# Spreading 28 groups of background slabs over eight loop iterations instead of seven, in a one-layer RWKV and block-attention step

## The chip, the core and the metric

The kernel runs on one core of a Trainium2 chip. The metric is the device time of one execution in microseconds (us). TensorE (PE) does the matmuls, with its weight loads (PEld) beside them; VectorE (DVE) and ScalarE (ACT) do the elementwise work and move results out of PSUM; GpSimd (POOL) does a little; SyncE (SP) issues nearly all DMAs, in program order.

## The reference, cut to what matters

One decoder layer is computed for 288 tokens (256 of a prompt, 8 sequences of 4). The normalised input `h` (288 x 2048) goes through one projection whose columns are split:

```
h = _rmsnorm(x, norm1_g) * (1 + scale1) + shift1       # scale, shift, gate: silu(c) @ w_ada
z = h @ w_in                                           # columns: z_a | q_b k_b v_b | gate_a gate_b
o_a = rwkv7(z_a) @ w_proj_a                            # 16 heads of 64, state recurrence
o_b = moba(rope(q_b), rope(k_b), v_b, cache) @ w_proj_b   # 8 heads of 128, paged keys and values
mix = sigmoid(gate_a) * o_a + sigmoid(gate_b) * o_b
x = x + gate1 * (mix @ w_out)                          # then a ConvFFN and a last norm
```

## The kernel before, in words

The stages run one after the other: adaLN and norm; `za` (the columns `z_a`); then eight iterations j = 0 to 7 of `rwkv(j)`, each for one pair of RWKV heads; then rotary and attention over the paged cache; then merge, out, up and down.

An RWKV iteration is a long chain of small steps that PE, ACT, DVE and POOL hand to each other (log decays, pair products, seven levels of a triangular inverse, two chunks of state, group norm). Two kinds of background work are threaded through it by hand, as every engine's order is the program's:

- **ada slabs.** `ada(j, p)`, p = 0 to 7, uses two 512 KB slabs of `w_ada` each, 16 per iteration, straight from the ring `raw`.
- **fill slabs.** The remaining 56 tiles of 128 columns of `w_in` (q_b, k_b, v_b, gates) are computed in 28 groups of two tiles. A group has four slabs of 512 KB. For each slab ACT makes `whi` (`rest_hi`), DVE makes `wlo` (`rest_lo`), and PE does 24 matmuls in two halves (`rest(j, i, 0)` and `rest(j, i, 1)`). After four slabs ACT copies two PSUM banks to `restev` (`rest_evac`) and stores them to `spill` in DRAM (`rest_spill`). `fill(i)` places slab i at its point of an iteration. Slabs 0 to 11 lie ahead of `ada(j, 6)`; slab 12 lies on both sides of the samples' state update, slab 13 around the turning of the final states, slab 14 around the two sums of the group norm, slab 15 at the very end.

Iterations 0 to 6 are `dense`: 4 groups, 16 fill slabs. Iteration 7 has none. Fill and ada slabs share the four places of the ring (fill in 1 and 3, ada in 0 and 2) in iterations 0 to 6; iteration 7 uses all four for ada. `rest_hi(j, RS)` and `rest_lo(j, RS)` prepare the next iteration's slab 0 near the end of an iteration, for j < 6.

An ada slab's load waits until the slab two before it is used. At an iteration's end the DVE does, in order: group norm's centring and squares (L1712, L1713), `fill(15)`, the next pair's `mix_pair`, then a reciprocal and four products, `yalo` (`ya_lo`), a small add to `mod`, the next slab's `rest_lo`, and then the next iteration's `v_kk` and `v_sq` (L1601, L1602). The next iteration on PE begins with four matmuls on `lora` and one pair on `v_sq`, ahead of its fill slab 0.

In iteration 7 SP also loads what attention needs first. The gates (32 of the spilled tiles, 4 DMAs, L740) are put where `hhi` and `hlo` lay, so they wait for the last fill slab; key pages 4 to 7 (L722) are put where `whi` and `wlo` lie, behind the last ada slab; `pair_stores` stores the pair's states (L694, L697). After the loop SP waits for `ya_lo`, for all the state stores and for the gates, and loads the heads' q, k and v from `spill` (`heads_load`, L747 and L748); `rotate(0)` on PE waits for the first head.

Of the kernel before, what the change touches and what calls it, by code (L numbers as in the profile page):

```python
# [31 lines left out]
P = 128  # L32
# [6 lines left out]
DB, HB, HEAD_B = 1024, 8, 128  # L39
KA = DA // P  # L40
# [14 lines left out]
CH = 512  # L55
# [77 lines left out]
def build(nc, d):  # L133
    ctx = ExitStack()
    with ctx:  # L135
# [397 lines left out]
        ADA_J = (ADA_G - ADA_1) // KA * ADA_K  # L533
        assert ADA_J == 16
        N_XT, N_T = 2 * LEVELS - 3, 2 * LEVELS - 2
        ADA_ROWS1 = 1
# [50 lines left out]
        def _(sp):  # L587
# [86 lines left out]
            def rest_slab(j, i):  # L674
                r, n = 1 + 2 * (i % 2), stages["rest"][0] + i
                src = d["w_in"][i % 4 * CH:i % 4 * CH + CH, bass.ds(j * (RG * RW) + (ZA + i // 4 * RW), RW)].rearrange("(t p) n -> p t n", p=P)
                sp.wait_ge(slab_lo, j * RS + (n - 1))
                sp.dma_start(quads(raw[:, r, :, :]), src).then_inc(slab_in[r], 16)

            def both_slabs(j, s0, s1):  # L680
                for s in range(s0, s1):
                    rest_slab(j, s)
                    ada_slab(j, s)
# [14 lines left out]

            with sp.Fori(0, 1) as j:
                both_slabs(j, 0, 3)  # L700
                lora_loads(j)
                both_slabs(j, 3, 13)
                state_loads(j)
                both_slabs(j, 13, RS)
            with sp.Fori(1, KA - 1) as j:
                both_slabs(j, 0, 3)
                lora_loads(j)
                both_slabs(j, 3, 6)
                pair_stores(j - 1)
                both_slabs(j, 6, 13)  # L710
                state_loads(j)
                both_slabs(j, 13, RS)

# [9 lines left out]

            j = KA - 1
            n1 = stages["merge"][0]
            for s in range(ADA_J):
                idx = ADA_1 * ADA_K + j * ADA_J + s
                src = wsrc(d["w_ada"], s % ADA_K * 2 * P, j * (2 * CH) + (ADA_1 + s // ADA_K) * CH, CH)
                if s < 4:
                    wait = ((ada_used, idx - 1), (slab_lo, n1 - 1), (ada_used, idx - 2), (slab_lo, n1))[s]  # L730
                else:
                    wait = (ada_used, idx - 3)
                slab(s, 0, 0, src, wait)
                if s == 5:
                    pair_stores(j - 1)
                if s == 9:
                    sp.wait_ge(spilled, 16 * RG * (KA - 1))
                    sp.wait_ge(slab_used, n1)
                    for q in range(4):
                        sp.dma_start(gt[:, 8 * q:8 * q + 8, :], spill[3 * HB + 8 * q:3 * HB + 8 * q + 8, :, :].rearrange("t p f -> p t f")).then_inc(reloaded, 16)  # L740
            sp.wait_ge(states_in, 48)
            pages("cache_k", 0, None, None, range(4, NPG))
            pair_stores(KA - 1)

# [68 lines left out]
        def landed(name, g, s):  # L813

            n0, ks, _ = stages[name]
            up0 = stages["up"][0]
            n = n0 + ks * g.c + s
            before = (ADA_1 if name == "za" else ADA_G) * ADA_K - ADA_RAW
            v, per = 16 * (before // 4 + n // 4 + 1), 4
            if name == "up":  # L820
                v, per = v + 16 * ((n - up0) // 4 + 1), 8
            if name == "down":
                v += 16 * (stages["down"][0] - up0) // 4
            return v if g.i is None else g.i * (g.a * ks * per) + v
# [114 lines left out]
        def _(act):  # L939
# [110 lines left out]
            def rest_hi(j, i):  # L1050
                r, n = 1 + 2 * (i % 2), stages["rest"][0] + i
                act.wait_ge(slab_in[r], j * (RS * 8) + 16 * (REST_IN + i // 2 + 1))
                act.wait_ge(slab_used, j * RS + (n - 1))
                copy(whi[:, n % 2, :, :], raw[:, r, :, :]).then_inc(slab_hi, 1)

            def rest_evac(j, q):
                act.wait_ge(slab_used, j * RS + (stages["rest"][0] + 4 * q + 4))
                act.wait_ge(spilled, j * (16 * RG) + 16 * q)
                copy(restev[:, :, :], ps[:, 5:7, 0:T]).then_inc(rest_out, 1)

            def rest_spill(j, q):
                act.wait_ge(rest_out, j * RG + (q + 1))
                act.dma_start(spill[one(j, 2, 2 * RG, 2 * q), :, :].rearrange("t p f -> p t f"), restev[:, :, :]).then_inc(spilled, 16)

# [4 lines left out]

            def rwkv(j, dense, more):  # L1070
                jc = one(j)
                w0h, a0h = smallc[:, one(j)], smallc[:, one(j, off=8)]

                def fill(i):
                    if dense:
                        rest_hi(j, i)
# [29 lines left out]
                copy(BN[0:m, 2, :], pbank(4)[0:m, 2 * P:3 * P], scale=-1.0).then_inc(rows_done, 1)  # L1106
                if dense:
                    rest_evac(j, 0)
                fill(5)

                for lev in range(1, LEVELS):
# [9 lines left out]
                    if lev == LEVELS - 1:  # L1121
                        act.wait_ge(t_done, j * N_T + N_T - 1)
                        for h in (slice(0, 64), slice(64, P)):
                            copy(Tf[h, :, :, h].rearrange("p e c t -> p (e c) t"), TT[h, :, :, :].rearrange("p e c t -> p (e c) t"))
                    if lev == 1 and dense:
                        rest_spill(j, 0)
                    if lev == 4 and dense:
                        rest_evac(j, 1)
                    if lev == 5 and dense:
                        rest_spill(j, 1)  # L1130
# [29 lines left out]
                right_sides(1)  # L1160
                if dense:
                    rest_evac(j, 2)
                fill(13)
                solved(1)
                if dense:
                    rest_spill(j, 2)
                fill(14)
# [13 lines left out]
                act.activation(v_px[:, :], pbank(0)[:, 0:T], ACT.Sqrt, bias=c("eps_lnx"), scale=1.0 / HEAD_A).then_inc(gn_roots, 1)  # L1181
                if more:
                    rest_hi(j, RS)
                act.wait_ge(ya_done, j + 1)
                act.activation(yahi[:, jc, :].rearrange("p o t -> p (o t)"), v_thw[:, :], ACT.Copy).then_inc(branch_hi, 1)
                if dense:
                    rest_evac(j, 3)
                    rest_spill(j, 3)
# [5 lines left out]
            for j in range(KA):  # L1194
                rwkv(j, j < KA - 1, j < KA - 2)

# [162 lines left out]
        def _(dve):  # L1359
# [227 lines left out]
            def rest_lo(j, i):  # L1587
                r, n = 1 + 2 * (i % 2), stages["rest"][0] + i
                dve.wait_ge(slab_hi, j * RS + (n + 1))
                TTn(wlo[:, n % 2, :, :], raw[:, r, :, :], whi[:, n % 2, :, :].bitcast(F32), ALU.subtract).then_inc(slab_lo, 1)  # L1590

            def rwkv(j, dense, more):

                def fill(i):
                    if dense:
                        rest_lo(j, i)
# [130 lines left out]
                ada_cols(2 * j + (ADA_1 + 1), 2 * j + (ADA_1 + 2), 7)  # L1727
                if more:
                    rest_lo(j, RS)

# [3 lines left out]
            for j in range(KA):  # L1734
                rwkv(j, j < KA - 1, j < KA - 2)

# [232 lines left out]
        def _(pe):  # L1969
# [178 lines left out]
            def ada(j, p):  # L2148

                for s in (2 * p, 2 * p + 1):  # L2150
                    if s % ADA_K == 0:
                        pe.wait_ge(ada_in_mod, 2 * j + (ADA_1 + s // ADA_K))
                    if isinstance(j, int) and j == KA - 1:
                        r = s % 4
                        pe.wait_ge(slab_in[r], 16 * (REST_IN + 8 * j + s // 4 + 1))
                    else:
                        r = 2 * (s % 2)
                        pe.wait_ge(slab_in[r], j * (RS * 8) + 16 * (REST_IN + s // 2 + 1))
                    for kt in range(2):
                        t = 2 * (s % ADA_K) + kt  # L2160
                        strip = slice(ADA_W * (t % 4), ADA_W * (t % 4) + ADA_W)
                        i = mm(pbank(7)[strip, :], scT[:, t, :], raw[:, r, kt, :], t < 4, t >= KD - 4)
                    i.then_inc(ada_used, 1)

            def rest(j, i, half):

                n = stages["rest"][0] + i
                if half == 0:
                    pe.wait_ge(slab_lo, j * RS + (n + 1))
                    if i % 4 == 0:  # L2170
                        pe.wait_ge(rest_out, j * RG + i // 4)
                wh, wl = quads(whi[:, n % 2, :, :]), quads(wlo[:, n % 2, :, :])
# [10 lines left out]

            def rwkv(j, dense):

                def fill(i, half):
                    if dense:
                        rest(j, i, half)
# [258 lines left out]
            for j in range(KA):  # L2447
                rwkv(j, j < KA - 1)

# [227 lines left out]
```

## Time and profile before

| | us |
|---|---|
| median of 3 runs (2392.01 to 2397.01) | 2396.04 |
| the profiled execution | 2395.43 |
| its span | 2393.6 |
| RWKV iterations 0 to 6, mean | 101.8 |
| iteration 7 (from 984.50) to `rotate(0)` at 1060.99 | 76.5 |

Times in a view are counted from the span's start. An iteration is named by its j, 0 to 7. In a timeline a row is one group of like instructions: start, length, engine, line, operation, output and inputs; in square brackets how long the engine sat idle before it and what it waited for. A matmul's length contains the time for its result to drain, so the distance of two starts tells more.

### The profile page before, as it was taken

The page shows a single profiled execution, that of the slowest core. Times are in us where ns is not written, and L with a number is a line of the kernel's source. Part 1 is how long each engine was busy: PE and PEld are TensorE (multiplying, and loading weights), DVE is VectorE, ACT ScalarE, POOL GpSimd, SP SyncE. Part 2 cuts the span into 40 slices and gives each one's busy share as a digit, 9 for nine tenths or more (in the row PEclk, how much of TensorE's full clock was granted, in tenths as well). Part 3 has the DMA queues.
Part 4 walks back from the last instruction along what each step waited for, and adds up shares of the span by engine and source line. Part 5 has one row for each costly group of instructions (what it writes and reads, how often), then busy time and mean ns, then how long its engine had stood idle before and what let it go on. Part 6 is the DMA issues. An engine that isn't in the chain of part 4 may idle for free. (4 is left out here: it accounts for less than half of the span.)

```text
span 2393.6 us, 49529 instructions
## 1 busy us (share of the span) xinstructions
PE 2282.3 (95%) x19772; PEld 2018.1 (84%) x19772; DVE 1150.5 (48%) x1904; ACT 959.4 (40%) x1413; POOL 105.5 (4%) x224
## 2 busy tenths in 40 slices
PE   6999899999999999878998999799999999999998
PEld 3889787887878788646666999799999999999998
DVE  4456635445353543434444555655544554544443
ACT  2433424334333343326452333354545545433333
POOL 0000011000000000100000000000100100000000
PEclk8999999999999999969998999999999999999999
DMA  9885556565665656667995455355555555555543
GB/s 332 307 290 147 159 182 184 177 196 179 187 189 177 183 177 190 216 207 252 390 384 185 150 161 166 98 167 167 165 163 163 165 167 166 163 166 164 160 149 117
DMA packets 326691, 461.20 MB, mean 193 GB/s; under 512 B 37337, under 2 KB 220395, under 8 KB 326075
## 3 DMA queue, kind: packets, MB, share of 16 engines
q1 hardware_dynamic: 318312, 450.22, 58.5%
q10 hardware_dynamic: 8215, 8.59, 1.1%
q8 instruction: 128, 2.10, 0.4%
q14 instruction: 36, 0.29, 0.0%
HBM read 442.86 MB, written 15.86 MB: 192 GB/s over the span
## 5 line engine op out<-in xcount | busy, mean ns | idle before, releaser
L942 ACT ACTIVATE whi<-raw 128x1024 fp32r<-128x1024 f32 (+1 forms) x512 | 526.3, 1028 | 910.8 <-PE ps L1973 880.9
L1973 PE MATMUL ps<-hhi,whi 128*128 128x288 f32 x2736 | 832.2, 304 | 10.0 <-DVE hlo L1456 6.4
L1973 PE MATMUL ps<-hhi,wlo 128*128 128x288 f32 x2736 | 807.9, 295 | 0.0
L1973 PE MATMUL ps<-hlo,whi 128*128 128x288 f32 x2736 | 807.2, 295 | 0.0
L1405 DVE TENSOR_TENSOR wlo<-raw,whi 128x1024 fp32r<-128x1024 f32 (+1 forms) x400 | 470.2, 1177 | 639.2 <-ACT whi L942 639.1
L1973 PEld LDWEIGHTS ps<-hhi,whi 128*128 128x128 f32 x2736 | 514.8, 188 | 72.5 <-issue 52.0
L1973 PEld LDWEIGHTS ps<-hlo,whi 128*128 128x128 f32 x2736 | 515.3, 188 | 1.2
L1973 PEld LDWEIGHTS ps<-hhi,wlo 128*128 128x128 f32 x2736 | 514.8, 188 | 0.0
L1973 PE MATMUL ps<-fhi,whi 128*128 128x288 f32 x704 | 208.0, 295 | 2.8 <-DVE wlo L1405 2.8
L1973 PE MATMUL ps<-fhi,wlo 128*128 128x288 f32 x704 | 207.7, 295 | 0.0
L1973 PE MATMUL ps<-flo,whi 128*128 128x288 f32 x704 | 207.3, 294 | 0.0
L1590 DVE TENSOR_TENSOR wlo<-raw,whi 128x1024 fp32r<-128x1024 f32 x112 | 136.7, 1220 | 101.8 <-ACT whi L942 101.6
L1973 PEld LDWEIGHTS ps<-fhi,whi 128*128 128x128 f32 x704 | 132.1, 188 | 3.6 <-DVE wlo L1405 3.5
L1973 PEld LDWEIGHTS ps<-flo,whi 128*128 128x128 f32 x704 | 132.1, 188 | 0.2
L1973 PEld LDWEIGHTS ps<-fhi,wlo 128*128 128x128 f32 x704 | 132.1, 188 | 0.0
L1973 PE MATMUL ps<-raw,scT 128*32 128x512 f32 x512 | 79.5, 626 | 5.6 <-DMA raw<-in_w_ada 5.6
L1973 PE MATMUL ps<-mhi,whi 128*128 128x288 f32 x256 | 76.4, 298 | 1.6 <-DVE wlo L1405 1.6
L942 ACT ACTIVATE Xs<-ps 128x256 f32<-128x256 f32 (+1 forms) x48 | 18.4, 383 | 143.3 <-PE ps L1973 143.1
L1973 PE MATMUL ps<-mlo,whi 128*128 128x288 f32 x256 | 75.7, 296 | 0.0
L1973 PE MATMUL ps<-mhi,wlo 128*128 128x288 f32 x256 | 75.2, 294 | 0.0
L942 ACT ACTIVATE kT<-ps 128x1024 f32<-128x1024 f32 x64 | 64.6, 1021 | 25.9 <-PE ps L2516 25.7
L1674 DVE TENSOR_TENSOR Tn<-Tn,ps 128x128 f32<-128x128 f32 x40 | 11.5, 288 | 122.2 <-PE ps L1973 122.2
(393 smaller groups left out, 2758.1 us busy)
## 6 DMA issues: line engine op xcount, KB each, us to landing
raw<-in_w_up SPq DMA_DIRECT2D x352, 256.0 KB, 2.9
raw<-in_w_ada SPq DMA_DIRECT2D x128, 512.0 KB, 4.8
raw<-in_w_in SPq DMA_DIRECT2D x112, 512.0 KB, 4.5
raw<-in_w_down SPq DMA_DIRECT2D x88, 512.0 KB, 3.8
kpage<-in_cache_v SPq DMA_DIRECT2D x64, 512.0 KB, 5.8
raw<-in_w_in SPq DMA_DIRECT2D x72, 384.0 KB, 5.6
kpage<-in_cache_k SPq DMA_DIRECT2D x40, 512.0 KB, 5.3
ada_d<-in_w_ada SPq DMA_DIRECT2D x32, 512.0 KB, 5.8
```

What stands on the lines that cost most here:

```text
L942: return act.activation(o, i, ACT.Copy, **k)
L1405: TTn(wlo[:, n % 2, :, 0:width], raw[:, n % 4, :, 0:width], whi[:, n % 2, :, 0:width].bitcast(F32), ALU.subtract).then_inc(slab_lo, 1)
L1590: TTn(wlo[:, n % 2, :, :], raw[:, r, :, :], whi[:, n % 2, :, :].bitcast(F32), ALU.subtract).then_inc(slab_lo, 1)
L1674: TTn(even, even, pbank(1)[:, 0:2 * H].rearrange("p (n t) -> p n t", t=1 << lev), ALU.subtract).then_inc(t_done, 1)
L1973: return pe.matmul(out, lhsT, rhs, start=start, stop=stop, **k)
```

## The change

`GROUPS = [4, 3, 4, 3, 4, 3, 4, 3]` gives the groups of each iteration. Odd iterations, the last among them, have fill slabs 0 to 11 only; the total stays 28. The counts of all semaphores follow. SP's two loops become one unrolled loop over all eight iterations; iteration 7 has the same ring places as the others. Gates and key pages 4 to 7 are issued after iteration 7's last ada slab, the pages first, once the last fill slab is used and spilled. The next iteration's slab 0 is prepared for all j < 7.

```diff
+        GROUPS = [4, 3, 4, 3, 4, 3, 4, 3]
+        G_0 = [sum(GROUPS[:j]) for j in range(KA + 1)]
...
             def both_slabs(j, s0, s1):
                 for s in range(s0, s1):
-                    rest_slab(j, s)
+                    if s < 4 * GROUPS[j]:
+                        rest_slab(j, s)
                     ada_slab(j, s)
...
-            with sp.Fori(0, 1) as j:
...
-            with sp.Fori(1, KA - 1) as j:
+            for j in range(KA):
                 both_slabs(j, 0, 3)
-                lora_loads(j)
+                if j < KA - 1:
+                    lora_loads(j)
                 both_slabs(j, 3, 6)
-                pair_stores(j - 1)
+                if j:
+                    pair_stores(j - 1)
                 both_slabs(j, 6, 13)
-                state_loads(j)
-                both_slabs(j, 13, RS)
+                if j < KA - 1:
+                    state_loads(j)
+                both_slabs(j, 13, ADA_J)
...
-            for s in range(ADA_J):
...
-                if s == 9:
-                    sp.wait_ge(spilled, 16 * RG * (KA - 1))
-                    sp.wait_ge(slab_used, n1)
-                    for q in range(4):
-                        sp.dma_start(gt[:, 8 * q:8 * q + 8, :], spill[3 * HB + 8 * q:3 * HB + 8 * q + 8, :, :].rearrange("t p f -> p t f")).then_inc(reloaded, 16)
             sp.wait_ge(states_in, 48)
+            sp.wait_ge(slab_used, stages["merge"][0])
             pages("cache_k", 0, None, None, range(4, NPG))
+            sp.wait_ge(spilled, 16 * G_0[KA])
+            for q in range(4):
+                sp.dma_start(gt[:, 8 * q:8 * q + 8, :], spill[3 * HB + 8 * q:3 * HB + 8 * q + 8, :, :].rearrange("t p f -> p t f")).then_inc(reloaded, 16)
             pair_stores(KA - 1)
...
                 def fill(i):
-                    if dense:
+                    if i < 4 * GROUPS[j]:
                         rest_hi(j, i)
...
-                if more:
-                    rest_hi(j, RS)
+                if j < KA - 1:
+                    rest_hi(j + 1, 0)
...
-                if dense:
+                if GROUPS[j] > 3:
                     rest_evac(j, 3)
                     rest_spill(j, 3)
```

DVE and PE get the same `if i < 4 * GROUPS[j]` for `fill`.

## Rows read from the trace of the kernel before

**Rows 1.** The page: TensorE's granted clock in 40 slices of the span.

```profile
PEclk8999999999999999969998999999999999999999
```

**Rows 2.** Windows: length, busy time by engine, then granted clock, DMA share, GB/s.

```profile
883.18:984.50 101.32, 99.92 (x1016) 82.07 (x1015) 46.38 (x85) 36.38 (x66) 6.94 (x11) 1.00 0.61 186
886.14:963.33 77.19, 76.64 (x853) 63.68 (x854) 33.09 (x60) 28.15 (x54) 5.27 (x10) 1.00 0.63 188
...
986.54:1038.42 51.88, 43.41 (x567) 28.76 (x566) 17.87 (x47) 14.14 (x39) 5.46 (x12) 0.83 0.80 264
1038.42:1061.00 22.58, 12.78 (x62) 6.51 (x58) 7.86 (x16) 4.28 (x7) 0.00 (x0) 0.65 0.20 50
1004.00:1024.00 20.00, 16.19 (x282) 12.33 (x284) 4.80 (x15) 4.69 (x12) 2.45 (x5) 0.83 1.06 357
```

**Rows 3.** Timeline of PE: marks of iterations 6 and 7 and the attention's start.

```profile
886.14 0.75 PE L1973 MATMUL ps<-v_sq,cst 128*128 128x288 f32 x2 [0.85 <-DVE v_sq L1602]
...
986.54 0.75 PE L1973 MATMUL ps<-v_sq,cst 128*128 128x288 f32 x2
...
1038.42 1.98 PE L1973 MATMUL ps<-Vblk,KN 32*64 32x512 f32 x4
...
1060.99 2.26 PE L1973 MATMUL ps<-qk,cst 128*128 128x288 f32 x4 [8.76 <-DMA vq<-spill]
```

**Rows 4.** Timeline of PE: iteration 6 behind `ada(6, 6)`.

```profile
965.12 1.08 PE L1973 MATMUL ps<-Vblk,KN 32*64 32x512 f32 x4
...
966.99 0.34 PE L1973 MATMUL ps<-VN,KN 128*64 128x64 f32 x4
...
969.10 0.40 PE L1973 MATMUL ps<-hhi,whi 128*128 128x288 f32 x1
...
972.40 0.27 PE L2428 MATMUL ps<-cst,SE 128*64 128x128 f32 x1
...
973.47 1.07 PE L1973 MATMUL ps<-raw,scT 128*32 128x512 f32 x8
...
976.17 0.65 PE L1973 MATMUL ps<-v_thw,cst 128*128 128x288 f32 x2
```

**Rows 5.** Timeline of DVE: ends of iterations 5 and 6.

```profile
884.10 1.22 DVE L1590 TENSOR_TENSOR wlo<-raw,whi 128x1024 fp32r<-128x1024 f32 x1
...
885.63 0.46 DVE L1602 TENSOR_TENSOR v_sq<-v_kk 128x288 f32<-128x288 f32 x1
...
977.35 0.46 DVE L1713 TENSOR_TENSOR v_sq<-v_ld 128x288 f32<-128x288 f32 x1
...
978.86 0.48 DVE L1561 SCALAR_TENSOR_TENSOR rkv<-dif,par,za 128x256 f32<-128x256 f32 x1
...
980.53 1.95 DVE L1718 RECIPROCAL v_px<-v_px 128x288 f32<-128x288 f32 x1
...
985.31 0.19 DVE L1397 TENSOR_TENSOR mod<-ps,par 128x36 f32<-128x36 f32 x1
```

**Rows 6.** Timeline of PE: iteration 0 starts after an idle stretch.

```profile
271.90 1.33 PE L1973 MATMUL ps<-lw,lora 64*128 64x288 f32 x4 [4.64 <-ACT nshn L942]
...
281.42 0.27 PE L2204 MATMUL ps<-cst,v_ld 128*128 128x128 f32 x1
```

**Rows 7.** Timeline of SP: its DMA issues.

```profile
963.56 0.37 SPq L672 DMA_DIRECT2D raw<-in_w_ada  x1
...
1003.88 8.52 SPq L740 DMA_DIRECT2D gt<-spill  x4
...
1048.56 5.16 SPq L697 DMA_DIRECT2D out_wkv_sample<-stout  x8
...
1056.90 0.83 SPq L747 DMA_DIRECT2D qk<-spill  x2
```

**Rows 8.** DMA issues from 984 to 1062: KB each, median us to landing.

```profile
raw<-in_w_ada SPq DMA_DIRECT2D x12, 512.0 KB, 4.7
gt<-spill SPq DMA_DIRECT2D x4, 1152.0 KB, 12.9
```

More of the change, by code:

```diff
@@ L534, in build @@
         assert ADA_J == 16
+        GROUPS = [4, 3, 4, 3, 4, 3, 4, 3]
+        G_0 = [sum(GROUPS[:j]) for j in range(KA + 1)]
+        assert G_0[KA] == RG * (KA - 1)
         N_XT, N_T = 2 * LEVELS - 3, 2 * LEVELS - 2
@@ L675, in rest_slab @@
                 r, n = 1 + 2 * (i % 2), stages["rest"][0] + i
-                src = d["w_in"][i % 4 * CH:i % 4 * CH + CH, bass.ds(j * (RG * RW) + (ZA + i // 4 * RW), RW)].rearrange("(t p) n -> p t n", p=P)
-                sp.wait_ge(slab_lo, j * RS + (n - 1))
+                src = d["w_in"][i % 4 * CH:i % 4 * CH + CH, bass.ds(ZA + (G_0[j] + i // 4) * RW, RW)].rearrange("(t p) n -> p t n", p=P)
+                sp.wait_ge(slab_lo, 4 * G_0[j] + (n - 1))
                 sp.dma_start(quads(raw[:, r, :, :]), src).then_inc(slab_in[r], 16)
@@ L697, in pair_stores @@
                     sp.dma_start(d["wkv_sample"][b, one(j, 2, 2), :, :].rearrange("h v k -> v h k"), stout[:, b, :, :]).then_inc(sstate_out, 16)
-            with sp.Fori(0, 1) as j:
+            for j in range(KA):
                 both_slabs(j, 0, 3)
-                lora_loads(j)
-                both_slabs(j, 3, 13)
-                state_loads(j)
-                both_slabs(j, 13, RS)
-            with sp.Fori(1, KA - 1) as j:
-                both_slabs(j, 0, 3)
-                lora_loads(j)
+                if j < KA - 1:
+                    lora_loads(j)
                 both_slabs(j, 3, 6)
-                pair_stores(j - 1)
+                if j:
+                    pair_stores(j - 1)
                 both_slabs(j, 6, 13)
-                state_loads(j)
-                both_slabs(j, 13, RS)
+                if j < KA - 1:
+                    state_loads(j)
+                both_slabs(j, 13, ADA_J)
             def pages(cache, R, used, value, which=range(NPG), apart=False):
@@ L722, in pages @@
                     sp.dma_start(place, d[cache][bass.ds(page, 1), :, :, :].rearrange("o p h f -> p (o h f)")).then_inc(landed_, 16)
-            j = KA - 1
-            n1 = stages["merge"][0]
-            for s in range(ADA_J):
[L727 to L735, printed above, removed]
-                if s == 9:
-                    sp.wait_ge(spilled, 16 * RG * (KA - 1))
-                    sp.wait_ge(slab_used, n1)
-                    for q in range(4):
-                        sp.dma_start(gt[:, 8 * q:8 * q + 8, :], spill[3 * HB + 8 * q:3 * HB + 8 * q + 8, :, :].rearrange("t p f -> p t f")).then_inc(reloaded, 16)
             sp.wait_ge(states_in, 48)
+            sp.wait_ge(slab_used, stages["merge"][0])
             pages("cache_k", 0, None, None, range(4, NPG))
+            sp.wait_ge(spilled, 16 * G_0[KA])
+            for q in range(4):
+                sp.dma_start(gt[:, 8 * q:8 * q + 8, :], spill[3 * HB + 8 * q:3 * HB + 8 * q + 8, :, :].rearrange("t p f -> p t f")).then_inc(reloaded, 16)
             pair_stores(KA - 1)
@@ L819, in landed @@
             v, per = 16 * (before // 4 + n // 4 + 1), 4
+            if name != "za":
+                v += 16 * (KA * ADA_J // 2 - 2 * G_0[KA]) // 2 * (1 if n % 2 == 0 else -1)
             if name == "up":
@@ L1051, in rest_hi @@
                 r, n = 1 + 2 * (i % 2), stages["rest"][0] + i
-                act.wait_ge(slab_in[r], j * (RS * 8) + 16 * (REST_IN + i // 2 + 1))
-                act.wait_ge(slab_used, j * RS + (n - 1))
+                act.wait_ge(slab_in[r], 16 * (REST_IN + 2 * G_0[j] + i // 2 + 1))
+                act.wait_ge(slab_used, 4 * G_0[j] + (n - 1))
                 copy(whi[:, n % 2, :, :], raw[:, r, :, :]).then_inc(slab_hi, 1)
             def rest_evac(j, q):
-                act.wait_ge(slab_used, j * RS + (stages["rest"][0] + 4 * q + 4))
-                act.wait_ge(spilled, j * (16 * RG) + 16 * q)
+                act.wait_ge(slab_used, stages["rest"][0] + 4 * (G_0[j] + q) + 4)
+                act.wait_ge(spilled, 16 * (G_0[j] + q))
                 copy(restev[:, :, :], ps[:, 5:7, 0:T]).then_inc(rest_out, 1)
             def rest_spill(j, q):
-                act.wait_ge(rest_out, j * RG + (q + 1))
-                act.dma_start(spill[one(j, 2, 2 * RG, 2 * q), :, :].rearrange("t p f -> p t f"), restev[:, :, :]).then_inc(spilled, 16)
+                act.wait_ge(rest_out, G_0[j] + q + 1)
+                act.dma_start(spill[one(G_0[j] + q, 2, 2), :, :].rearrange("t p f -> p t f"), restev[:, :, :]).then_inc(spilled, 16)
             def ada_rows2(j, half):
@@ L1068, in ada_rows2, with rwkv @@
                 copy(adr[:, :], pbank(7)).then_inc(ada_copied, 1)
-            def rwkv(j, dense, more):
+            def rwkv(j):
                 jc = one(j)
@@ L1106, in rwkv @@
                 copy(BN[0:m, 2, :], pbank(4)[0:m, 2 * P:3 * P], scale=-1.0).then_inc(rows_done, 1)
-                if dense:
-                    rest_evac(j, 0)
+                rest_evac(j, 0)
                 fill(5)
@@ L1124, in rwkv @@
                             copy(Tf[h, :, :, h].rearrange("p e c t -> p (e c) t"), TT[h, :, :, :].rearrange("p e c t -> p (e c) t"))
-                    if lev == 1 and dense:
+                    if lev == 1:
                         rest_spill(j, 0)
-                    if lev == 4 and dense:
+                    if lev == 4:
                         rest_evac(j, 1)
-                    if lev == 5 and dense:
+                    if lev == 5:
                         rest_spill(j, 1)
@@ L1160, in rwkv @@
                 right_sides(1)
-                if dense:
-                    rest_evac(j, 2)
+                rest_evac(j, 2)
                 fill(13)
                 solved(1)
-                if dense:
-                    rest_spill(j, 2)
+                rest_spill(j, 2)
                 fill(14)
@@ L1181, in rwkv @@
                 act.activation(v_px[:, :], pbank(0)[:, 0:T], ACT.Sqrt, bias=c("eps_lnx"), scale=1.0 / HEAD_A).then_inc(gn_roots, 1)
-                if more:
-                    rest_hi(j, RS)
+                if j < KA - 1:
+                    rest_hi(j + 1, 0)
                 act.wait_ge(ya_done, j + 1)
                 act.activation(yahi[:, jc, :].rearrange("p o t -> p (o t)"), v_thw[:, :], ACT.Copy).then_inc(branch_hi, 1)
-                if dense:
+                if GROUPS[j] > 3:
                     rest_evac(j, 3)
@@ L1194, in _ @@
             for j in range(KA):
-                rwkv(j, j < KA - 1, j < KA - 2)
+                rwkv(j)
             def plain(name, u=None, added=None, ends={}):
@@ L1588, in rest_lo, with rwkv @@
                 r, n = 1 + 2 * (i % 2), stages["rest"][0] + i
-                dve.wait_ge(slab_hi, j * RS + (n + 1))
+                dve.wait_ge(slab_hi, 4 * G_0[j] + (n + 1))
                 TTn(wlo[:, n % 2, :, :], raw[:, r, :, :], whi[:, n % 2, :, :].bitcast(F32), ALU.subtract).then_inc(slab_lo, 1)
-            def rwkv(j, dense, more):
+            def rwkv(j):
                 def fill(i):
-                    if dense:
+                    if i < 4 * GROUPS[j]:
                         rest_lo(j, i)
@@ L1727, in rwkv @@
                 ada_cols(2 * j + (ADA_1 + 1), 2 * j + (ADA_1 + 2), 7)
-                if more:
-                    rest_lo(j, RS)
+                if j < KA - 1:
+                    rest_lo(j + 1, 0)
             own(dve.memset(Tf[64:P, :, :, 0:64], 0.0))
@@ L1734, in _ @@
             for j in range(KA):
-                rwkv(j, j < KA - 1, j < KA - 2)
+                rwkv(j)
             def fl(ap):
@@ L2152, in ada @@
                         pe.wait_ge(ada_in_mod, 2 * j + (ADA_1 + s // ADA_K))
[L2153 to L2158, printed above, removed]
+                    r = 2 * (s % 2)
+                    pe.wait_ge(slab_in[r], 16 * (REST_IN + j * (ADA_J // 2) + s // 2 + 1))
                     for kt in range(2):
@@ L2168, in rest @@
                 if half == 0:
-                    pe.wait_ge(slab_lo, j * RS + (n + 1))
+                    pe.wait_ge(slab_lo, 4 * G_0[j] + (n + 1))
                     if i % 4 == 0:
-                        pe.wait_ge(rest_out, j * RG + i // 4)
+                        pe.wait_ge(rest_out, G_0[j] + i // 4)
                 wh, wl = quads(whi[:, n % 2, :, :]), quads(wlo[:, n % 2, :, :])
@@ L2182, in rest, with rwkv @@
                     ins.then_inc(slab_used, 1)
-            def rwkv(j, dense):
+            def rwkv(j):
                 def fill(i, half):
-                    if dense:
+                    if i < 4 * GROUPS[j]:
                         rest(j, i, half)
@@ L2447, in _ @@
             for j in range(KA):
-                rwkv(j, j < KA - 1)
+                rwkv(j)
+            pe.wait_ge(rest_out, G_0[KA])
             pe.wait_ge(ya_lo, KA)
```

## The prediction, made before the changed kernel ran

> **What bounds the kernel now.** I read the page's slices first, then windows over single iterations, then the timelines of PE, DVE and SP around the places that the change touches. The slices [rows 1] show TensorE at its full clock nearly everywhere, with one dip in the middle. The windows place it: iteration 6 runs at clock 1.00 with PE busy for 99.9 of 101.3 us, while in iteration 7 the clock is 0.83 and PE is busy for 43.4 of 51.9 us up to the mark of 1038.42, and then 0.65 and 12.8 of 22.6 us up to the start of attention [rows 2]. So the dense iterations are bound by PE's queue of work, and the one without fill slabs by its own chain of small steps, partly at half clock. Moving PE work into iteration 7 fills that hole. The question is what the iterations that give it up lose, and what the later loads cost.
>
> Three marks divide the time. V(j) is the start of the `v_sq` matmuls at an iteration's beginning, at 886.14 for j = 6 and 986.54 for j = 7 [rows 3]. A(j) is the end of `ada(j, 6)`: behind it the fill slabs 12 to 15 are placed; it is 963.33 for j = 6 [rows 2] and 1038.42 for j = 7 [rows 3]. R is the distance from A(7) to `rotate(0)`, 1060.99 - 1038.42 = 22.6 us now [rows 3].
>
> **Step 1, iteration 7 gets twelve fill slabs.** V to A becomes as long as in iteration 6, whose first twelve slabs are the same: 77.2 us in place of 51.9 [rows 2], so +25.3 us. Twelve slabs at 3.3 us (two halves from 969.10 to 972.40 [rows 4]) are 39.6 us of PE work, so about 14 us of it go into idle time and slow clock. This is the whole gain of the change.
>
> **Step 2, slab 0 of iteration 7.** The end of iteration 6 now prepares it as the ones before did. In iteration 6 PE waited 0.85 us for DVE's `v_sq` [rows 3], 2.96 us after the iteration's start at 883.18 [rows 2]; iteration 7 reached the mark 2.04 us after 984.50. That is +0.9 us.
>
> **Step 3, the three tails without slabs 12 to 15 (j = 1, 3, 5).** Now A(6) to the next V takes 984.50 - 963.33 + 2.96 = 24.1 us. What it takes without fill is a chain through three engines, which I lay out from A. The samples' update on PE takes 966.99 - 965.12 = 1.9 us, chunk results 969.10 - 966.99 = 2.1, turning the states 973.47 - 972.40 = 1.1, `ada(j, 7)` another 1.1 [rows 4]: 6.2 us. The load of the last ada slab goes out about 0.9 us after A (the one before it leaves 0.23 after A, at 963.56 [rows 7]) and lands 4.7 us later [rows 8], at 5.6 us; PE wants it at about 5.7, so it may be just late, by a few tenths. Group norm: from the first sum's matmul at 976.17 [rows 4] to the end of DVE's squares at 977.81 [rows 5] are 1.6 us: 7.8. `mix_pair` takes 980.53 - 978.86 = 1.7 (PE's second sum and ACT's root lie beside it): 9.5. Reciprocal to `mod`, 985.31 - 980.53 = 4.8: 14.3. Then 0.1 for `mod`, and from the start of the next `rest_lo` to the end of `v_sq` 886.09 - 884.10 = 2.0 [rows 5]: 16.4 us, and with a tenth for the ada slab 16.5. PE's own work ends earlier: the next V is set by DVE, and PE stands some 4 us idle ahead of it, having only the `lora` matmuls to do. So a tail saves 24.1 - 16.5 = 7.6 us, though it gives up 12.9 us of PE work (21.2 us of the tail less its own 8.3 of small steps). I take 7.5, three times: -22.5 us. The bounds are 6.5 (the ada slab a full microsecond late) and 12.9 (no new stall). The evacuation and spill that fall away lie beside PE and cost nothing either way; SP's unrolling changes no order.
>
> **Step 4, from A(7) to attention.** Before, gates and key pages were loaded beside iteration 7. Now SP can send them only after the last ada slab's load, 0.9 us after A. Behind A stand two ada slabs (1.05 MB), four pages of 512 KB (2.1 MB) and the gates, 4 x 1152 KB = 4.72 MB [rows 8]: 7.9 MB. While the gates were loaded before, all DMA engines were busy and moved 357 GB/s [rows 2], so this takes 22.0 us and ends at about A + 23 to 24, with the time in which the first bytes come into motion. The last state stores are issued behind the gates; SP needs 5.2 us for them [rows 7] and they are done at about A + 24.3. The heads' loads wait for both, and `rotate(0)` came 1060.99 - 1056.90 = 4.1 us after the first of them was issued [rows 3, 7]. So R becomes 28.4 us, +5.8. Compute alone would be ready earlier: `ya_lo` comes at about A + 13.8 (7.8, then 1.2 for sum and root, 4.8 for the DVE's products), so R is at least 17.9. The upper bound is 32, if SP cannot issue its stores before the queue has drained (its four gate issues took 8.5 us before [rows 7]) and stores and landing follow the gates in series.
>
> The pattern speaks against spreading as such: an iteration of 4 groups hides its chain fully; one of 3 loses 5.3 us (12.9 - 7.6), and four such lose 21 us, whereas the empty iteration lost about 17 (the 76.5 us to `rotate(0)` less the 8.8 us of idle time before it [rows 3] are 67.7; an iteration's own steps without fill and waits are about 101.3 - 4 x 12.9 = 50).
>
> **Rivals.**
>
> *The clock falls in the short tails.* Each has an idle stretch of some 4 us behind light work. Iteration 0 shows what that costs: after 4.64 us idle, 9.5 us pass from its first matmul to the transposes of `v_ld` [rows 6], where 2.0 + 0.8 + 3.3 = 6.1 are needed at full clock. That is 3.4 us, three times: +10.3, 2415 us. For it: that one gap is of the size expected here. Against it: the stretch V to A of iteration 7, light work all through, still had a mean clock of 0.83 [rows 2], and a short tail is much shorter. I give it 0.2. The Trainium skill ("TensorE: Matmul & The Clock Gate", Why this matters for your kernels) warns of idle gaps between bursts of matmuls, behind which the clock is low again; by that rule this is the likely case and the sum would be 2415. The trace agrees in the one place that has such a gap.
>
> *The later loads are hidden.* If the transfers end before `ya_lo`, R is 17.9 in place of 28.4. The total is 9.5 - 10.5 = -1.0: 2394 us, no difference. It needs 7.9 MB in 13 us, about 600 GB/s, against 357 seen; or that the heads don't wait for the gates, which the code excludes. Chance 0.12.
>
> *The tails cost nothing.* If DVE's chain overlapped with the next iteration's first slab and PE never waited, each tail would save all 12.9 us: 25.3 + 0.9 - 38.7 + 5.8 = -6.7, 2389 us, faster. It decides from 10.7 us saved per tail on, that is a new stall below 2.2 us. Against it stands the order of PE's queue, where fill slab 0 lies behind the matmuls on `v_sq`, and that even the dense tail is 0.85 us short [rows 3]. Chance 0.09.
>
> That the change does nothing is no case: it moves 12 slabs.
>
> **How the numbers follow.** The case above has a chance of 0.55, with its own range from 2400 (tails save 8.5, R 26.5) to 2411 (6.5 and 31). The clock has 0.2, the hidden loads 0.12, the free tails 0.09, and 0.04 is left for what I don't see, more of it slow. The range 2395 to 2416 leaves out the free tails, part of the hidden loads, and the worst of the clock case. A measurement of this kernel tells about 0.2% (4.8 us) from no change. Within it fall the hidden loads and the lower edge of the main case, 0.15; faster 0.1; slower 0.75.
>
> **What would show it.** Right: distance V to V of 101 us for even j and 94 for j = 1, 3, 5; PE idle for 4 us or more ahead of the `v_sq` matmuls in iterations 2, 4 and 6, put down to DVE's L1602; A(7) at about 986.5 + 0.9 - 22.5 + 77.2 = 1042, 4 us later than before; DMA engines full for 20 us behind it; `rotate(0)` at about 1070 after an idle stretch of more than 15 us, put down to the heads' DMA. Wrong: short tails of 89 to 91 us (free), or of 97 and more with a clock below 1.00 (throttled); `rotate(0)` less than 20 us behind A(7); or a change of length behind `rotate(0)`, on which I set nothing.

## The result, and the profile after

The changed kernel takes 2407.98 us (median of 4 runs, 2402.84 to 2413.03) against 2394.3 us of the kernel before, run beside it. The ratio is 1.0055, with a 95% interval of 1.0040 to 1.0071: slower by 0.55%, where 0.4% had been forecast (2405 us). The profiled execution is the fastest of the four, 2402.84 us with a span of 2401.0 us, 7.4 us above the profiled one of before. Its V(0) also lies 3.5 us earlier than in the trace shown before (272.15 against 275.68), ahead of everything that the change touches, so the distances between marks tell more than the totals.

Windows of the changed kernel: iterations 1 and 2 from V to V, V to A of iteration 7, A(7) to `rotate(0)`, and 20 us inside that. They answer to [rows 2].

```profile
375.28:468.78 93.50, 87.31 (x918) 69.33 (x918) 41.53 (x82) 33.31 (x63) 8.04 (x11) 0.98 0.58 175
468.78:571.28 102.50, 101.24 (x1015) 83.21 (x1015) 46.20 (x85) 36.96 (x66) 8.04 (x11) 0.99 0.60 184
965.05:1040.65 75.60, 75.60 (x854) 63.55 (x854) 30.54 (x58) 26.23 (x52) 6.56 (x12) 1.00 0.53 166
1040.65:1071.66 31.01, 8.49 (x61) 4.77 (x58) 7.87 (x16) 4.17 (x7) 0.00 (x0) 0.68 0.92 297
1044.00:1064.00 20.00, 5.14 (x35) 3.11 (x32) 6.54 (x15) 4.17 (x7) 0.00 (x0) 0.70 1.06 360
```

Iteration 7 is now filled: 75.6 us at full clock with PE never idle. Iteration 1, with three groups, lasts 93.5 us and PE is busy for 87.3 of them. Behind A(7) PE has 8.5 us of work in 31.0 us, while the DMA engines are full.

Timeline of PE from A(1), at 452.21, over the bare end of iteration 1, and around A(7) and `rotate(0)`; the latter two answer to [rows 3].

```profile
452.21 1.08 PE L1960 MATMUL ps<-Vblk,KN 32*64 32x512 f32 x4
...
460.32 0.75 PE L1960 MATMUL ps<-v_sq,cst 128*128 128x288 f32 x2 [1.04 <-DVE v_sq L1700]
460.91 0.95 PE L1960 MATMUL ps<-cst,adr 128*128 128x9 f32 x8
461.80 0.76 PE L1960 MATMUL ps<-lw,lora 64*128 64x288 f32 x4
...
468.78 1.33 PE L1960 MATMUL ps<-v_sq,cst 128*128 128x288 f32 x2 [4.87 <-DVE v_sq L1589]
...
1040.65 1.08 PE L1960 MATMUL ps<-Vblk,KN 32*64 32x512 f32 x4
...
1071.66 2.26 PE L1960 MATMUL ps<-qk,cst 128*128 128x288 f32 x4 [21.48 <-DMA vq<-spill]
```

From A(1) to V(2) pass 16.6 us. PE waits 4.87 us of them for DVE's `v_sq`, and the pair on it then takes 1.33 us in place of the 0.75 in [rows 3]: TensorE is at its lower clock (1.2 GHz). Windows of 1 us place the fall, first in the tail of iteration 1, then in that of iteration 3:

```profile
463.00:464.00 1.00, 0.91 (x3) 0.29 (x2) 0.96 (x2) 0.00 (x0) 0.00 (x0) 1.00 1.04 379
464.00:465.00 1.00, 0.00 (x0) 0.00 (x0) 0.93 (x3) 0.00 (x0) 0.00 (x0) 0.90 0.23 80
465.00:466.00 1.00, 0.00 (x0) 0.00 (x0) 0.71 (x2) 0.22 (x1) 0.00 (x0) 0.50 0.00 0
659.00:660.00 1.00, 1.00 (x6) 0.35 (x5) 1.00 (x3) 0.84 (x1) 0.00 (x0) 0.68 1.13 387
```

PE's wait begins at 463.9, and the clock falls about 1 us into it. In iteration 3 it falls between 659 and 660 with PE at work, some 3 us ahead of that tail's wait, which is then 3.37 us long. Timeline of DVE in the same stretch, which answers to [rows 5]:

```profile
459.81 0.46 DVE L1700 TENSOR_TENSOR v_sq<-v_ld 128x288 f32<-128x288 f32 x1
...
461.86 1.95 DVE L1705 RECIPROCAL v_px<-v_px 128x288 f32<-128x288 f32 x1
...
466.63 0.19 DVE L1384 TENSOR_TENSOR mod<-ps,par 128x36 f32<-128x36 f32 x1
466.74 1.22 DVE L1577 TENSOR_TENSOR wlo<-raw,whi 128x1024 fp32r<-128x1024 f32 x1
467.87 0.36 DVE L1588 TENSOR_SCALAR v_kk<-rkv,par 128x288 f32<-128x288 f32 x1
468.27 0.46 DVE L1589 TENSOR_TENSOR v_sq<-v_kk 128x288 f32<-128x288 f32 x1
```

From the start of the group norm's squares to the end of the next `v_sq`, 468.73, DVE has one gap, 0.51 us ahead of `yalo` for ACT's `yahi`, and otherwise none above a few hundredths: the wait is that chain. Timeline of SP behind A(7), which answers to [rows 7]:

```profile
1042.73 3.72 SPq L723 DMA_DIRECT2D kpage<-in_cache_k  x4
1046.49 9.98 SPq L730 DMA_DIRECT2D gt<-spill  x4
1056.52 3.23 SPq L698 DMA_DIRECT2D out_wkv_prompt<-stp  x1
1059.80 5.16 SPq L701 DMA_DIRECT2D out_wkv_sample<-stout  x8
1067.78 0.81 SPq L735 DMA_DIRECT2D qk<-spill  x2
```

The prompt state's store, which took 0.63 us to issue in the kernel before, takes 3.23 here, and the eight stores of the sample states go out at 1059.8, 19 us behind A. The heads' loads begin 27.1 us behind A.

| distance | before | after | forecast |
|---|---|---|---|
| V to V, j = 1, 3, 5 | 101.3, 101.3, 101.9 | 93.5, 94.8, 93.5 | 94 |
| V to V, j = 2, 4, 6 | 101.1, 101.6, 100.4 | 102.5, 102.4, 103.1 | 101 (j = 6: 101.3) |
| V(7) to A(7) | 51.9 | 75.6 | 77.2 |
| A(7) to `rotate(0)` | 22.6 | 31.0 | 28.4 |
| `rotate(0)` to the span's end | 1332.6 | 1329.4 | the same |

### The profile page after: what moved, and what is told of

It reads as the page before. It is cut to its first block and busy times, and to the rows that moved or that the text cites. A ratio compares the mean times of both kernels' runs of the same rounds, so it can differ in the third digit from the quotient of the medians.

```text
span 2401.0 us, 48785 instructions
## 1 busy us (share of the span) xinstructions
PE 2275.6 (95%) x19772; PEld 2015.8 (84%) x19772; DVE 1149.8 (48%) x1904; ACT 959.3 (40%) x1413; POOL 113.2 (5%) x224
## 5 line engine op out<-in xcount | busy, mean ns | idle before, releaser
L932 ACT ACTIVATE Xs<-ps 128x256 f32<-128x256 f32 (+1 forms) x48 | 18.4, 383 | 144.1 <-PE ps L1960 143.9
```

Of the source, the lines that this page charges most:

```text
L932: return act.activation(o, i, ACT.Copy, **k)
```

## The experiments

`all_in_seven`, `no_gates`, `warm` and `squares_early` ran beside 21 runs of the kernel before (median 2393.82 us), the other four beside 24 (2394.99 us).

**The groups of before with the loads of after.** `all_in_seven`:

```diff
-        GROUPS = [4, 3, 4, 3, 4, 3, 4, 3]
+        GROUPS = [4, 4, 4, 4, 4, 4, 4, 0]
...
```

The rest of the diff takes away the copies, the spills and the prepared slab 0 of a group that isn't there.

> The changed kernel with the groups of before (4 in seven iterations, none in the last): no short tail and no fill in iteration 7, but gates and first key pages still behind the last ada slab. Theory (the tails cost about 6 us each with the clock, the late loads about 8 us): iterations 0 to 6 last 101.3 us again, the A mark of iteration 7 is 52 to 58 us behind V, because its ada slabs now have two places in the ring, R is about 30 us in place of 22.6, and the kernel needs 2402 to 2409 us, slower than before by 8 us or more. Rival (the late loads are harmless, the short tails are the whole loss): 2393 to 2397 us, as before.

Measured: 2407.58 us, ratio 1.0051 (1.0034 to 1.0068). Windows from V(7) to A(7) and on to `rotate(0)`:

```profile
981.67:1044.51 62.84, 52.81 (x566) 37.06 (x565) 17.89 (x47) 14.16 (x39) 5.46 (x12) 0.65 0.35 110
1044.51:1075.84 31.33, 13.15 (x61) 6.49 (x58) 7.87 (x16) 4.28 (x7) 0.00 (x0) 0.61 0.88 287
```

R is 31.3 us without any fill in iteration 7 and without a short tail: the late loads cost 8.7 us by themselves. V to A is longer than expected, 62.8 us: against [rows 2] PE is busy 9.4 us more with the same 566 matmuls, at a mean clock of 0.65 in place of 0.83. Iterations 1 to 5 last 100.6 to 101.4 us. So the loss of the late loads is real and separate, and an empty last iteration is worse beside them than it was. The trace shows where that begins. The same stretch in three windows, and the instruction that holds up DVE, and PE behind it, in the second:

```profile
981.67:997.00 15.33, 12.03 (x129) 7.10 (x128) 9.18 (x21) 7.72 (x19) 2.07 (x6) 1.00 0.57 166
997.00:1001.00 4.00, 1.07 (x11) 0.16 (x8) 1.44 (x5) 0.00 (x0) 0.21 (x1) 0.91 0.51 114
1001.00:1044.51 43.51, 39.71 (x429) 29.80 (x429) 7.27 (x22) 6.44 (x20) 3.18 (x6) 0.50 0.27 89
```

```profile
999.56 1.42 DVE L1644 TENSOR_TENSOR Rm<-ps,cst 128x256 f32<-128x256 f32 x4 [3.99 <-DMA out_wkv_sample<-stout]
```

DVE waits 3.99 us for the stores of the pair before, which SP issues behind the iteration's first six ada slabs; PE then stands idle for 3.97 us, and the clock is at 0.50 from there to A(7). In the trace of before DVE doesn't wait at that place. The sample states' stores go out 10.4 us behind V(7) here, against 4.8 before, when the ada slabs had four places in the ring and not two. So the ring places have a part in it; no run takes them back alone.

**One short tail.** `one_short`:

```diff
-        GROUPS = [4, 3, 4, 3, 4, 3, 4, 3]
+        GROUPS = [4, 4, 4, 4, 4, 4, 3, 1]
...
```

> The changed kernel with groups 4, 4, 4, 4, 4, 4, 3, 1: one short tail, and one group in the last iteration. Theory: iterations 1 to 5 last 101.3 us, iteration 6 about 93.7, iteration 7 loses 0.5 to 1.5 us at half clock at its start, its V to A lasts 66 to 70 us (its first four slabs, then the small steps with the ada slabs in two places), R is 31 as in the changed kernel. The total is that of the groups-as-before kernel less 13 us for the group moved out of iteration 6, plus 5 to 6 for the tail, plus 4 to 8 in iteration 7: 2403 to 2410. Rival (the loss is that of the late loads alone and short tails are free): below 2400.

Measured: 2405.2 us, ratio 1.0046 (1.0031 to 1.0060).

```profile
879.57:972.64 93.07, 87.16 (x918) 69.32 (x919) 41.57 (x82) 33.31 (x63) 6.90 (x11) 0.99 0.58 176
972.64:1039.85 67.21, 62.93 (x662) 46.98 (x662) 21.14 (x50) 16.50 (x41) 5.46 (x12) 0.75 0.38 119
```

Iterations 1 to 5 are back at 100.8 to 101.3 us and the one short iteration lasts 93.1: the loss belongs to each short tail and not to the change as a whole. R is 30.2 us.

**Without the gates' loads.** `no_gates` leaves them out, with the waits on them lowered to match. The sigmoids read the layer's input in their place, so the outputs are not the layer's:

```diff
-            for q in range(4):
-                sp.dma_start(gt[:, 8 * q:8 * q + 8, :], spill[3 * HB + 8 * q:3 * HB + 8 * q + 8, :, :].rearrange("t p f -> p t f")).then_inc(reloaded, 16)
...
```

> The changed kernel without the four loads of the gates; the sigmoids read the layer's input in their place, so the merge gets other factors. Theory (the heads wait behind 4.7 MB of gates): R falls from 31 to 18 to 22 us, and the kernel gains 9 to 13 us, to about 2396. Rival (R is set by the state stores' own wait and by SP's issuing of pages and stores): R stays above 26, and the gain is below 5 us.

Measured: 2394.14 us, ratio 1.0011 (0.9997 to 1.0025). R is 18.4 us:

```profile
1041.41:1059.85 18.44, 8.55 (x62) 4.79 (x58) 7.86 (x16) 4.17 (x7) 0.00 (x0) 0.77 0.77 244
```

SP issues the sample states' stores at 1048.0, 6.6 us behind A in place of 19.2, and the heads at 1055.9. So the gates' 4.7 MB are the whole of the loss behind A: R is 12.6 us shorter than in the changed kernel, and near the 17.9 that the prediction gave as the least.

**Idle matmuls in the wait.** `warm` puts 32 matmuls whose result is overwritten ahead of the `v_sq` pair behind each short tail:

```diff
+                if j and GROUPS[j - 1] < 4:
+                    pe.wait_ge(rest_out, G_0[j])
+                    for _ in range(32):
+                        mm(pbank(5)[:, 0:T], hhi[:, 0, 0:P], hhi[:, 1, :])
                 pe.wait_ge(kk_squares, j + 1)
```

> The changed kernel with 32 idle matmuls on PE (into the bank of the next fill group, overwritten later) in the wait ahead of v_sq behind each short tail: some 4.3 us of work in a 4.9 us wait. Theory (the idle stretch brings the clock to half for a few us, which costs 1.3 us in each following iteration): the clock stays at 1.00 there, iterations 2, 4 and 6 last 101.3 in place of 102.6 us, and the kernel gains 3 to 4 us, about 2403 to 2405. Rival (the longer even iterations have another cause, such as a later slab): their length stays at 102.6 with the clock at 1.00.

Measured: 2399.52 us, ratio 1.0023 (1.0013 to 1.0032). Timeline of PE, and the two iterations' windows:

```profile
463.58 4.52 PE L1960 MATMUL ps<-hhi 128*128 128x288 f32 x32
468.52 0.75 PE L1960 MATMUL ps<-v_sq,cst 128*128 128x288 f32 x2 [0.42 <-DVE v_sq L1589]
```

```profile
375.07:468.52 93.45, 91.99 (x950) 73.61 (x950) 41.53 (x82) 33.35 (x63) 8.07 (x11) 1.00 0.57 175
468.52:569.78 101.26, 99.93 (x1014) 82.08 (x1014) 46.23 (x85) 36.97 (x66) 6.94 (x11) 1.00 0.61 186
```

The short iteration keeps its length, since DVE sets it; the clock stays at 1.00 up to A(7), the pair takes 0.75 us again, and the even iterations last 101.3, 101.0 and 101.1 us in place of 102.5, 102.4 and 103.1. That is 1.2, 1.4 and 2.1 us, 1.6 on average and 4.7 in all. The whole gained 7.7 us by the ratios (0.32%), more than the 3 to 4 expected, and the two intervals leave 2 to 14 us. From V(0) to V(7) the two traces differ by 5.8 us, so a further 1.1 lies in the other iterations, most of it in iteration 3; the rest I can't place, and the changed kernel's runs lie 10 us apart.

**DVE's order.** `squares_early`:

```diff
                 if j < KA - 1:
                     mix_pair(j, 1)
+                    dve.wait_ge(gn_vars, j + 1)
+                    kk_start(j + 1)          # v_kk and v_sq of the next pair
+                    rest_lo(j + 1, 0)
                 dve.wait_ge(gn_roots, j + 1)
...
-                if j < KA - 1:
-                    rest_lo(j + 1, 0)
```

> The changed kernel with one order changed on DVE: the next pair's v_kk and v_sq and the next fill slab 0's low part come right behind mix_pair, ahead of the reciprocal and the four products. Theory (the short tail is set by DVE's chain ahead of v_sq): the 4.9 us wait of PE ahead of the v_sq matmuls goes, about 1 us of it comes back at v_ld, a short iteration lasts 89 to 91 us in place of 93.9, the clock no longer falls behind it, the dense boundaries lose their 0.85 us; all in all 13 to 18 us less, about 2391. Rival (the tail is set by the ada slabs' loads or by the sum of many small waits): short iterations stay within 1 us of 93.9 and the gain is 0.85 us per boundary at most, 5 us in all.

Measured: 2415.07 us, ratio 1.0089 (1.0072 to 1.0106): slower, against both expectations. The longest waits of PE over the RWKV stage and into attention, in us: total, number, longest one.

```profile
PE ps L1964 <- DMA vq<-spill: 23.5, 3, 21.5
PE ps L1964 <- DVE wlo L1577: 15.1, 7, 2.7
...
PE ps L2191 <- DVE v_ld L1594: 3.7, 3, 3.3
```

The wait ahead of `v_sq` is gone at all seven boundaries, and a wait for slab 1's low part has taken its place at all seven. Timelines of DVE, ACT and PE at the start of iteration 2 show why:

```profile
470.33 0.46 DVE L1718 TENSOR_TENSOR yalo<-v_thw,yahi 128x288 fp32r<-128x288 f32 x1 [0.51 <-ACT yahi L1172]
...
476.04 1.23 DVE L1577 TENSOR_TENSOR wlo<-raw,whi 128x1024 fp32r<-128x1024 f32 x1 [1.14 <-ACT whi L932]
```

```profile
470.87 1.28 ACT L1070 ACT_TABLE_LOAD   x1 [0.57 <-DVE yalo L1718]
472.16 0.50 ACT L1070 ACTIVATE v_thw<-ps,smallc 128x288 f32<-128x288 f32 x1
...
474.96 1.05 ACT L932 ACTIVATE whi<-raw 128x1024 fp32r<-128x1024 f32 x1
```

```profile
473.06 0.33 PE L2191 MATMUL ps<-cst,v_ld 128*128 128x128 f32 x1 [0.20 <-DVE v_ld L1594]
477.32 0.40 PE L1964 MATMUL ps<-hhi,whi 128*128 128x288 f32 x1 [2.72 <-DVE wlo L1577]
```

ACT's tanh must wait for `yalo`, because both use `v_thw`; slab 1's `whi` is queued behind tanh and root on ACT. Moving two products and a slab ahead of `yalo` made that path 2 us later: `yalo` begins 8.6 us behind the group norm's squares in place of 6.5. Every boundary has the wait, 2.0 us behind a dense iteration and 1.5 to 2.7 behind a short one. The short iteration did shrink, 93.5 to 92.85 us, and the next one grew from 102.5 to 105.5; the mark between them moved, so their sum tells more, 198.3 us in place of 196.0. V(7) to A(7) grew too, from 75.6 to 80.1. The wait had two loops through DVE behind it, and the edit relieved one at the cost of the other.

The clock fell here as well, and not behind a long wait. At the end of iteration 1 PE has stood idle for 1.04 us only, up to 462.29:

```profile
464.00:465.00 1.00, 1.00 (x5) 0.56 (x4) 0.95 (x3) 0.52 (x1) 0.00 (x0) 0.73 1.10 392
465.00:466.00 1.00, 1.00 (x3) 0.29 (x2) 1.00 (x2) 0.00 (x0) 0.00 (x0) 0.50 1.04 376
```

It also fell behind five of the seven waits for slab 1, three of them 2.0 us long at the start of iterations 1, 3 and 7.

**Other slabs left out.** `spread` keeps the last slabs in iterations 1, 3 and 5 and leaves out positions 6, 8, 10 and 12; the evacuation of the second group moves to where slab 12 was on ACT, and that of the third to the iteration's end:

```diff
+        KEEP = [list(range(16)) if g == 4 else [0, 1, 2, 3, 4, 5, 7, 9, 11, 13, 14, 15] for g in GROUPS]
+        KEEP[KA - 1] = list(range(12))
...
-                    if i < 4 * GROUPS[j]:
-                        rest(j, i, half)
+                    if i in KEEP[j]:
+                        rest(j, KEEP[j].index(i), half)
...
```

> The changed kernel, but iterations 1, 3 and 5 leave out fill positions 6, 8, 10 and 12 in place of 12 to 15: the same twelve slabs, with three of them at the end over DVE's chain. Theory (a short iteration loses 5 to 7 us only because its end is bare): a short iteration lasts 89 to 91 us in place of 93.9, PE waits 0.85 us ahead of v_sq as behind a dense one, the clock stays at 1.00 and the even iterations are back at 101.3; 12 to 18 us less than the changed kernel, 2390 to 2395. Rival (any four slabs left out expose as much, since the engines' small steps bind everywhere once PE has less to do): short iterations stay at 93 us or more, with waits at the places left out, and the time stays above 2402.

Measured: 2392.01 us, ratio 0.9996 (0.9978 to 1.0014), the time of the kernel before. The two windows of iterations 1 and 2, and PE's waits over the RWKV stage and into attention:

```profile
375.12:464.67 89.55, 87.23 (x919) 69.48 (x919) 41.45 (x81) 32.54 (x62) 8.59 (x11) 1.00 0.60 183
464.67:566.69 102.02, 99.92 (x1015) 82.08 (x1015) 46.28 (x85) 37.43 (x67) 8.06 (x11) 1.00 0.60 184
```

```profile
PE ps L1968 <- DMA vq<-spill: 22.5, 3, 21.1
PE ps L1968 <- DVE v_sq L1597: 5.9, 7, 0.8
PE ps L1968 <- DMA raw<-in_w_ada: 4.7, 8, 1.3
...
PE ps L1968 <- ACT Xs L934: 1.4, 3, 0.5
```

With the same number of slabs the short iterations last 89.6, 93.3 and 90.3 us, mean 91.1 in place of 93.9, the wait ahead of `v_sq` is 0.8 us as in a dense iteration, and the four places left out cost a wait of 0.5 us (`Xs`) and one of 0.2 in each short iteration. The even iterations lost their dip. Iteration 3 is the exception: it lies 2.9 to 3.7 us above the other two, and the clock is low in it from 637.8 to 644.7, among the samples' matmuls behind A(3), with no wait ahead of the fall but one of 0.72 us for an ada slab. At half clock PE loses about 3.4 us in that time, which is the difference. In `spread_heads` iteration 3 is again the long one (94.9 us against 89.8 and 90.0), so this is no chance of one trace.

**Gates behind the heads.** `heads_first`:

```diff
             pages("cache_k", 0, None, None, range(0, 4))
+            for q in range(4):
+                sp.dma_start(gt[:, 8 * q:8 * q + 8, :], spill[3 * HB + 8 * q:3 * HB + 8 * q + 8, :, :].rearrange("t p f -> p t f")).then_inc(ada_x_in[3], 16)
             pages("cache_k", 1, keys_turned, lambda p: p + 1)
...
                 keys(b + 1)
+                if b == 0:
+                    act.wait_ge(ada_x_in[3], ADA_X + 64)
+                gate(b)
                 outs(b)
...
```

The same four loads fall away behind iteration 7's key pages.

> The changed kernel with the gates' loads issued behind the heads and the first four key pages, and their sigmoids moved into the attention's loop, one for each sequence. Theory (attention waits for the gates' 4.7 MB only because they are ahead in the queue, and the queue is idle for 15 us behind the first pages): R falls from 31 to 18 to 21 us, the gates land in the rotary stretch unseen, 9 to 12 us less, about 2397. Rival (the bytes are paid anyway: the gates delay the pages that follow, or the sigmoids' table loads cost as much): R falls but the stretch from rotate(0) to the merge gets as much longer, and the time stays above 2403.

Measured: 2396.32 us, ratio 1.0003 (0.9994 to 1.0012).

```profile
1042.21:1059.79 17.58, 8.49 (x62) 4.77 (x58) 7.86 (x16) 4.17 (x7) 0.00 (x0) 0.82 0.77 244
1059.79:1085.00 25.21, 20.20 (x92) 13.06 (x93) 17.17 (x24) 6.70 (x28) 0.00 (x0) 0.79 1.05 359
```

R is 17.6 us, 13.4 less. The gates now fill the DMA engines in the rotary stretch, where the changed kernel used about half of them over the 25 us behind `rotate(0)` (0.54). Not all of it is free: from `rotate(0)` to the first merge matmul it takes 220.0 us (1059.79 to 1279.83) in place of 214.0 (1071.66 to 1285.66).

**Both.** `spread_heads`:

> Both edits of the two runs before together. If the two losses are separate, the gains add: 2407 less 15 less 10, about 2382, and the kernel is faster than before by 0.4 to 0.6%. If they share a cause the gain is no more than that of the larger one, 2392 or above.

Measured: 2383.55 us, ratio 0.9952 (0.9933 to 0.9971). Against the kernel before, the slow change has become one that is faster by 0.5%. The two gains alone were 0.0059 and 0.0052 of the ratio, together 0.0111, and both edits gain 0.0103: they add nearly in full, so the two losses were separate. The trace has both, short iterations of 89.8, 94.9 and 90.0 us and an R of 17.9.

## Why the prediction was right, point by point

**Step 1, filling iteration 7: right.** +23.7 us against +25.3. The stretch ran without any wait.

**Step 2, slab 0 of iteration 7: right**, a wait of 0.84 us there.

**Step 3, the short tails: right in mechanism and size.** A short iteration takes 93.9 us on average where 101.3 - 7.5 = 93.8 was worked out, and the wait ahead of `v_sq` was 4.87 us in two of three tails. The chain laid out link by link held too: 16.6 us from A(1) to V(2) against 16.5, with the reciprocal at 9.7 (9.5) and the add to `mod` at 14.4 (14.3). That the bare end is the cause, and not a missing group as such, is shown by `spread`; that it belongs to each tail, by `one_short`. What the step left to a rival is the clock. *The clock falls in the short tails* did come true, in all three, with a chance of only 0.2, but at 1.6 us each and not 3.4: the 3.4 us from [rows 6] had the clock at half for some 8 us behind the first matmuls of an iteration, here it was for 2.8, 3.5 and 5.6 us behind V(2), V(4) and V(6). `warm` takes the dip away and with it the 1.6 us. So the main case lacked a term of +4.7 us; the argument against the rival, that a short tail is much shorter than iteration 7, did not hold. What brings the clock down is less clear than the rival had it. The Trainium skill's warning of idle gaps ("TensorE: Matmul & The Clock Gate", Why this matters for your kernels) agrees with the trace in so far as the clock was at half behind all three gaps of 3.4 to 4.9 us. But in iteration 3 it had fallen before the gap, and in `squares_early` and `spread` it fell with no gap above 1.04 and 0.72 us ahead of it. These places share a stretch of small matmuls around and behind A; the gap alone isn't shown to be the cause.

**Step 4, from A(7) to attention: right in mechanism, too small.** +8.4 us against +5.8. The transfers went as worked out, at 360 GB/s. The sentence on the stores takes more from the Trainium skill ("DMA: Bandwidth & Descriptors", Queues, rings and completion order) than the page says, which also has a later transfer's write finish before an earlier one's; only the semaphore lands behind all earlier writes of its engine. Nothing in the sum rests on it, and no run separates it from SP's own delay. What was missed is SP: its pages began 2.1 us behind A in place of about 1.3, and it was held up in issuing gates and prompt store until 19 us behind A, so that the sample states' stores followed in series, and the heads began at A + 27.1 and not 24.3. The prediction had this as its upper bound, 32. `no_gates` and `heads_first` show that the gates' place in SP's order is the cause.

**Behind `rotate(0)`** nothing was set, and the traces differ by 3.3 us in the other direction, 1332.6 and 1329.4. The five other traces whose program is the changed one's from there on lie between 1330.7 and 1332.5, so much of this may be no more than one trace differs from the next.

**The whole: the number was helped by chance.** From V(0) to `rotate(0)` the traces show +14.2 us where +9.5 was summed. Of the 4.7 us missed, 4.0 are the even iterations with the clock's dips (+4.9 in place of +0.9) and 2.6 are R, less 1.6 us that iteration 7 was better. In the profiled execution, at 2402.84 us, 3.3 us behind `rotate(0)` and 3.5 ahead of V(0) then hid the shortfall. The medians do not hide it: they lie 13.7 us apart.

**The rivals.** *The later loads are hidden* is refuted by R. *The tails cost nothing* is refuted by the 4.87 us and by the 7.5 us that a tail saved. The remark that spreading loses to one empty iteration held only for slabs left out at the end. With the gates still late, `all_in_seven` (none spread) and the changed kernel take the same time.

## What to carry to other kernels

Background work that hides a chain of small steps is worth most where the chain is tightest, here at the loop's end. If an iteration must give some up, leave it out at places where the trace of an unfilled iteration shows waits of half a microsecond, not in a block at the end: with the same number of slabs left out a short iteration took 91.1 us or 93.9, and the clock's dip behind it besides. Before moving a load to a later place, add up all that then stands ahead of the next critical load in the same queue, and count the time that the issuing engine is held up as well as the bytes. And the instruction that an engine waits for isn't always the one to move: look for the second path that ends just behind it.

## What the hardware showed unexpectedly

- The granted clock fell to half at the end of all three short tails, but at no fixed place: about 1 us into PE's wait behind iteration 1, nearly 4 us into it behind iteration 5, and some 3 us before it in iteration 3, with PE at work. Each time 10 us or so of small matmuls stood ahead of the fall. In `squares_early` it fell there without a long wait. 32 matmuls without use in the gap, on the full array, kept it at full up to A(7). The useless work made the kernel faster: 1.0023 against 1.0055 of the kernel before.
- SP needed 3.23 us to issue one 32 KB store right behind the issue of 4.7 MB of gates, against 0.64 us in `no_gates` and `heads_first`, where they did not stand ahead of it.
- In `all_in_seven` the bare last iteration was 11 us longer than before, and 9.4 us of that are the same matmuls at a mean clock of 0.65 in place of 0.83. It begins with one wait of 4 us, for a store. The DMA engines were then less busy (0.35 against 0.80), which speaks against contention. Behind the wait the clock stayed at 0.50 for 43 us, although PE counted as busy for 39.7 of them.
